# Two transformer blocks on one core: the even attention takes short and long token tiles in another order

## The reference

```python
def diff_attend(q, k, v, lam):
    s = jnp.einsum('bqhmd,bkhmd->bhmqk', q, k) * (A_QK ** -0.5)
    p = jax.nn.softmax(s, axis=-1)
    a = p[:, :, 0] - lam * p[:, :, 1]
    return jnp.einsum('bhqk,bkhd->bqhd', a, v)
```

## Time and profile before

| | |
|---|---|
| median of 3 runs | 2235.92 us (2234.37 to 2238.08) |
| profiled execution, its span | 2237.9 us |
| mean granted clock of TensorE | 0.982 |
| busy in the span: TensorE | 2167.8 us (97%) |
| busy in the span: VectorE | 1361.6 us (61%) |
| busy in the span: ScalarE | 559.2 us (25%) |

### The profile page before, as it was taken

One profiled execution on the slowest core, in us unless ns is written; L12 is line 12 of the kernel. 1 busy time (PEld: TensorE's weight loads), 2 busy tenths in 40 slices (PEclk: granted clock), 3 DMA queues, 4 the chain that ended last, 5 costly groups with the idle time before them and its releaser, 6 DMA issues.

```text
span 2237.9 us, 28630 instructions
## 1 busy us (share of the span) xinstructions
PE 2167.8 (97%) x12022; PEld 1779.8 (80%) x12022; DVE 1361.6 (61%) x1795; ACT 559.2 (25%) x1105; POOL 48.7 (2%) x31
## 2 busy tenths in 40 slices
PE   8999998899999999999999999999999999999998
PEld 5788885568788668887888888888888888888887
DVE  5124547985571474885787754554888437977633
ACT  4110006861221462374311110221100003111101
POOL 0000000000010020300000000000000000000000
PEclk9899997999799999999999999999999999999999
DMA  7233322312131012202222222222222232222322
GB/s 308 98 127 119 126 65 59 82 61 95 36 126 63 33 57 75 77 18 95 76 94 98 105 82 91 97 95 103 84 83 74 99 101 87 100 88 99 110 94 76
DMA packets 34241, 204.54 MB, mean 91 GB/s; under 512 B 4801, under 2 KB 5057, under 8 KB 14657
## 3 DMA queue, kind: packets, MB, share of 16 engines
q1 hardware_dynamic: 32736, 197.99, 25.4%
q10 hardware_dynamic: 1376, 4.72, 0.6%
HBM read 191.16 MB, written 2.10 MB: 86 GB/s over the span
## 4 chain that ended last, share of the span: by engine, by line
PE 86%; DVE 8%; ACT 3%; issue 2%; DMA 1%; DVEq 0%; SPq 0%; ACTq 0%
PE ps L437 23%; PE ps L438 22%; PE ps L439 22%; PE ps L536 3%; PE ps L538 3%; PE ps L537 3%; PE ps L691 2%; DVE stat L2236 2%; PE ps L585 1%; PE ps L1332 1%; PE ps L568 1%; PE ps L791 1%; PE ps L1024 1%; DVE h2lo L2062 1%; ACT prob L1568 1%
## 5 line engine op out<-in xcount | busy, mean ns | idle before, releaser
L1940 DVE CAST whi<-raw 128x2048 fp32r<-128x2048 f32 (+2 forms) x148 | 172.2, 1164 | 440.2 <-DMA raw<-in_ffn_out 107.7
L437 PE MATMUL ps<-h2hi,whi 128*128 128x512 f32 (+1 forms) x1084 | 416.9, 385 | 3.4 <-DVE h2lo L2062 3.0
L439 PE MATMUL ps<-h2hi,wlo 128*128 128x512 f32 (+1 forms) x1084 | 412.6, 381 | 0.0
L438 PE MATMUL ps<-h2lo,whi 128*128 128x512 f32 (+1 forms) x1084 | 412.5, 381 | 0.0
L1943 DVE TENSOR_TENSOR wlo<-raw,whi 128x2048 fp32r<-128x2048 f32 (+2 forms) x148 | 320.2, 2164 | 5.1
L437 PE MATMUL ps<-h1hi,whi 128*128 128x512 f32 (+1 forms) x768 | 271.7, 354 | 3.4 <-DVE h1lo L2144 1.4
L438 PE MATMUL ps<-h1lo,whi 128*128 128x512 f32 (+1 forms) x768 | 269.5, 351 | 0.0
L439 PE MATMUL ps<-h1hi,wlo 128*128 128x512 f32 (+1 forms) x768 | 267.5, 348 | 0.0
L437 PEld LDWEIGHTS ps<-h2hi,whi 128*128 128x128 f32 x1084 | 203.7, 188 | 44.6 <-DVE h2lo L2062 3.0
L439 PEld LDWEIGHTS ps<-h2hi,wlo 128*128 128x128 f32 x1084 | 203.7, 188 | 39.3
L438 PEld LDWEIGHTS ps<-h2lo,whi 128*128 128x128 f32 x1084 | 203.8, 188 | 37.7
(11 more groups left out here) (330 smaller groups left out, 3333.3 us busy)
## 6 DMA issues: line engine op xcount, KB each, us to landing
raw<-in_ffn_in SPq DMA_DIRECT2D x44, 1024.0 KB, 4.9
raw<-in_even SPq DMA_DIRECT2D x16, 1024.0 KB, 7.8
mod_w<-in_mod SPq DMA_DIRECT2D x6, 2048.0 KB, 19.1
raw<-in_odd SPq DMA_DIRECT2D x12, 1024.0 KB, 4.9
raw<-in_sgu_v SPq DMA_DIRECT2D x12, 1024.0 KB, 4.8
raw<-in_sgu_u SPq DMA_DIRECT2D x12, 1024.0 KB, 4.9
raw<-in_sgu_out SPq DMA_DIRECT2D x16, 768.0 KB, 4.2
raw<-in_ffn_out SPq DMA_DIRECT2D x16, 704.0 KB, 4.0
```

The lines of the kernel that those rows point to most:

```text
L437: pe.matmul(o, r(lhi), r(rhi), start=first, stop=False, **kw)
L438: pe.matmul(o, r(lhi), r(rlo), start=False, stop=False, **kw)
L439: return pe.matmul(o, r(llo), r(rhi), start=False, stop=last, **kw)
L1940: step(dve.tensor_copy(whi[:, slot, 0:width].bitcast(F32R), raw[:, slot, 0:width]))
```

## The change

`EVEN_T` sets the order of tiles in a pair to 4, 0, 5, 1, 2, 3: two short units, two long ones, two short ones, six long ones. What was tied to a tile number is tied to the place in the pair (u % 12). `EVEN_SLOT` gives the place of a tile's result in bank 7, so that part 0 of the output copy (four tiles, now 4, 0, 5, 1) is one instruction that reads the places in another order, and part 1 takes tiles 2 and 3. `SUM_AT` keeps each unit's sum in its old column. The head sums go to bank 5, and are made with unit 4 of a pair; the first scores that use this bank again wait for the variance. The convolved parts go from the pair's unit 9 (the second head of tile 4, now gone from there) to unit 9 of the new order, and the variance to unit 4. The first scores wait for `zed`, the second for `sg_in`, the third for `b_read`, which was the wait of the first. As the last unit is long now, its early blocks are copied behind the loop.

```diff
@@ -310,7 +310,10 @@
         sg = {k: sem(f"sgu_{k}") for k in ("v", "moments", "root", "normed", "gelu", "gated",
                                            "rowsum", "ws", "rows_copied", "uhalf")}
 
-        EVEN_UNITS = [(hp, t, a) for hp in range(4) for t in range(6) for a in range(2)]
+        EVEN_T, EVEN_SLOT = (4, 0, 5, 1, 2, 3), (1, 0, 3, 2, 0, 1)
+        EVEN_UNITS = [(hp, t, a) for hp in range(4) for t in EVEN_T for a in range(2)]
+        long_units = [sum(t < 4 for _, t, _ in EVEN_UNITS[:u + 1]) for u in range(len(EVEN_UNITS))]
+        SUM_AT = [32 + 12 * hp + 2 * t + a for hp, t, a in EVEN_UNITS]
         EVEN_MOVES = [2 if t < 4 else 1 for _, t, _ in EVEN_UNITS]
         moved = [sum(EVEN_MOVES[:u]) for u in range(len(EVEN_UNITS) + 1)]
         ROPE = [(side, j) for j in range(4) for side in range(2)]
@@ -321,7 +324,7 @@
 
         def head_sums_at(t):
 
-            return ps[:, 2, 256:268] if t < 3 else ps[:, 6, 0:12]
+            return ps[:, 5, 256:268] if t < 3 else ps[:, 6, 0:12]
 
         WITH_PREV = [sum(1 for v in range(u) if v % 4) for u in range(17)]
         SWA_TILES = [u + WITH_PREV[u] for u in range(17)]
@@ -778,12 +781,14 @@
 
                 hp, t, a = EVEN_UNITS[u]
                 b = 3 * (u % 2)
-                if t == 0 and a == 0:
+                if u % 12 == 0:
                     pe.wait_ge(ea["stack"], 384 * (hp + 1))
                 if u >= 2:
                     pe.wait_ge(ea["exp"], 2 * (u - 1))
-                if t == 0 and a == 0 and hp >= 2:
-                    pe.wait_ge(ea["var"], hp - 1)
+                if u == 2:
+                    pe.wait_ge(b_read, 4)
+                if u % 12 == 7 and hp:
+                    pe.wait_ge(ea["var"], hp)
 
                 def term(o, m, i, k0, n):
                     rows = slice(64 * m, 64 * m + 64)
@@ -797,7 +802,7 @@
                             first.then_inc(ea["bank_shared"], 1)
                         term(ps[:, b + 2, :], 1, i, 256, 512)
                     term(ps[:, b, :], 0, 0, 0, 512)
-                    pe.wait_ge(ea["bank_shared"], 8 * hp + 2 * t + a + 1)
+                    pe.wait_ge(ea["bank_shared"], long_units[u])
                     for i in range(2):
                         term(ps[:, b + 1, 256:512], 1, i, 0, 256)
                     last = term(ps[:, b, :], 0, 1, 0, 512)
@@ -811,16 +816,17 @@
 
                 hp, t, _ = EVEN_UNITS[2 * p]
                 kts = (range(3 * half, 3 * half + 3), range(4 + half, 5 + half))[t >= 4]
+                slot = EVEN_SLOT[p % 6]
                 if half == 0:
                     pe.wait_ge(ea["copied"], moved[2 * p + 2])
-                    if t == 4:
+                    if p % 6 == 4:
                         pe.wait_ge(ea["out"], 2 * hp + 1)
-                    elif t == 0 and hp:
+                    elif p % 6 == 0 and hp:
                         pe.wait_ge(ea["out"], 2 * hp)
                 for kt in kts:
                     for a in range(2):
                         h = 2 * hp + a
-                        last = pe.matmul(ps[64 * a:64 * a + 64, 7, t % 4 * P:t % 4 * P + P], ev[:, kt, h * 64:h * 64 + 64],
+                        last = pe.matmul(ps[64 * a:64 * a + 64, 7, slot * P:slot * P + P], ev[:, kt, h * 64:h * 64 + 64],
                                          ept[(2 * p + a) % 4][:, kt, :], start=kt == (0 if t < 4 else 4), stop=kt == 5)
                 if half:
                     last.then_inc(ea["pv"], 1)
@@ -842,15 +848,16 @@
                                      blk[:, 0:P:64], start=True, stop=True)
                 last.then_inc(ea["sums"], 1)
 
-            pe.wait_ge(b_read, 4)
+            pe.wait_ge(zed, 4)
             even_scores(0)
+            pe.wait_ge(sg_in, 4)
             even_scores(1)
             pe.wait_ge(mod_ready, 8)
             last_unit = len(EVEN_UNITS) - 1
             for u, (hp, t, a) in enumerate(EVEN_UNITS):
                 if u < last_unit - 1:
                     even_scores(u + 2)
-                if (t, a) == (4, 0) and hp:
+                if u % 12 == 4 and hp:
                     head_sums(hp - 1, head_sums_at(hp - 1))
                 if u:
                     even_transposes(u - 1, range(4, 6), moved[u] - 1)
@@ -1567,7 +1574,7 @@
                 at = m * (TA if t < 4 else 512)
                 act.activation(prob[u % 3][:, m, 0:n], flat[:, at:at + n], ACT.Exp,
                                bias=stat[:, 2 * (u % 4) + m:2 * (u % 4) + m + 1],
-                               accum_out=stat[:, 8 + u % 4:9 + u % 4] if m else stat[:, 32 + u:33 + u])\
+                               accum_out=stat[:, 8 + u % 4:9 + u % 4] if m else stat[:, SUM_AT[u]:SUM_AT[u] + 1])\
                     .then_inc(ea["exp"], 1)
 
             def even_copy(u, late):
@@ -1583,8 +1590,12 @@
 
             def even_out(hp, part):
                 act.wait_ge(ea["pv"], 6 * hp + (4, 6)[part])
-                cols = (slice(0, TX), slice(TX, TA))[part]
-                tell(copy(eot[:, hp, cols], ps[:, 7, 0:(TX, TC)[part]]), ea["out"], 2 * hp + part + 1)
+                if part == 0:
+                    to = eot[:, hp, :].rearrange("p (j i n) -> p j i n", i=2, n=P)[:, 0:3:2, :, :]
+                    last = copy(to, ps[:, 7, :].rearrange("p (i j n) -> p j i n", i=2, n=P))
+                else:
+                    last = copy(eot[:, hp, 256:512], ps[:, 7, 0:256])
+                tell(last, ea["out"], 2 * hp + part + 1)
 
             even_exp(0, 0)
             even_exp(0, 1)
@@ -1598,13 +1609,14 @@
                     even_copy(u - 1, 1)
                 if u < last_unit:
                     even_exp(u + 1, 1)
-                if (t, a) == (0, 0) and hp < 3:
+                if u % 12 == 0 and hp < 3:
                     even_hi(hp + 1)
-                if (t, a) == (1, 0) and hp:
+                if u % 12 == 2 and hp:
                     even_out(hp - 1, 1)
                     even_square(hp - 1)
-                elif (t, a) == (5, 0):
+                elif u % 12 == 10:
                     even_out(hp, 0)
+            even_copy(last_unit, 0)
             even_copy(last_unit, 1)
             act.preload_act_table(ACT.Sqrt)
             even_out(3, 1)
@@ -2257,20 +2269,19 @@
                 i = u % 4
                 dve.wait_ge(ea["exp"], 2 * u + 2)
                 step(dve.reciprocal(stat[:, 12 + i:13 + i], stat[:, 8 + i:9 + i]))
-                step(dve.scalar_tensor_tensor(out=stat[:, 16 + i:17 + i], in0=stat[:, 32 + u:33 + u], scalar=lam4[:, 3:4],
+                step(dve.scalar_tensor_tensor(out=stat[:, 16 + i:17 + i], in0=stat[:, SUM_AT[u]:SUM_AT[u] + 1], scalar=lam4[:, 3:4],
                                               in1=stat[:, 12 + i:13 + i], op0=ALU.mult, op1=ALU.mult))
                 p = prob[u % 3]
                 dve.scalar_tensor_tensor(out=p[:, 0, 0:n], in0=p[:, 1, 0:n], scalar=stat[:, 16 + i:17 + i],
                                          in1=p[:, 0, 0:n], op0=ALU.mult, op1=ALU.add).then_inc(ea["probs"], 1)
                 if u + 2 < len(EVEN_UNITS):
                     even_max(u + 2)
-                if (t, a) == (0, 1) and hp < 3:
+                if u % 12 == 1 and hp < 3:
                     even_lo(hp + 1)
-                if (t, a) == (4, 1):
-                    if hp:
-                        head_variance(hp - 1)
-                    if hp < 2:
-                        convolved_parts(hp)
+                if u % 12 == 4 and hp:
+                    head_variance(hp - 1)
+                if u % 12 == 9 and hp < 2:
+                    convolved_parts(hp)
 
             convolved_parts(2)
             convolved_parts(3)
```

## The result

The changed kernel takes 2254.98 us (median of 6 runs; five lie between 2247.88 and 2258.48, the sixth took 4665.37 and is left out of the ratio) beside 2238.0 us for the kernel before on the same chip. The ratio is 1.0065 with a 95% interval of 1.0049 to 1.0081: slower by some 11 to 18 us. The forecast was 2240.6 us (2233 to 2246.5), so the direction was the expected one and the size was not. The profiled execution spans 2256.7 us with a mean granted clock of 0.977.

A forecast was written before the change was run, and what follows sets the result against it. VectorE was taken to set the pace of the even attention, with 11.1 us of waits to save at most. Waits -0.2, tail +3.1 and clock +1.8 gave +4.7 us on 2235.92: 2240.6 us, range 2233 to 2246.5.

The forecast's parts named there:

- clock, behind pair 0: Stage behind pair 0: one fall of TensorE's clock taken, +1.8 us, bounds 0 (none) and +8 (four).
- waits: VectorE's waits over the stage: 10.7 us after the change against 10.9 before, a gain of 0.2 us.
- tail, net of work done earlier: Stage end, now long units: 10.35 us to the first output product against 5.08, less 2.13: +3.1 us.
- the one at 385: In the kernel before: TensorE's 1.75 us wait next to the convolved parts, after which the clock fell.
- rival B: TensorE's work in thinner pieces, clock falls once a pair, four falls at about 2 us: 2247 us; chance 0.2.
- price for a fall: Ahead of the pair boundary 1.8 us against 0.83 before; after the first short couple, at the head sums, 2 to 2.3.
- the walk: Engine-by-engine timelines of the stage: 3.8 us of waits for start and pair 0, 2.05 each in pairs 1 to 3.
- First scores and moved work: Stage start: earlier scores win 0.26 us; convolved parts, variance, DMAs, weight loads and strided copy taken at no cost.
- the signs that were named: VectorE's wait for TensorE 2.6 to 6 or 7 us, for ScalarE 8.3 to 3 to 5; tail about 10 us.
- Rival A: Short couples find TensorE free, waits 4.2 in place of 10.9: 2232.3 us, 2229 if the end is overlapped; chance 0.22.

The follow-up runs named there:

- more fillers: Changed kernel plus repeated value products and scores and small filler products where TensorE waits, in pairs 0 to 2: 2247.18 us, ratio 1.0029.
- all remedies: Changed kernel with last pair in old order, convolved parts at the next pair's unit 4, fillers in pairs 0 to 2 except at unit 10: 2236.0 us.
- head sums behind: Changed kernel with the head sums issued behind the transposes and value product of their turn instead of ahead: 2250.95 us, ratio 1.0066.
- parts at unit 4: Changed kernel with the convolved parts of pairs 0 and 1 moved from unit 9 to unit 4 of the next pair: 2246.68 us, ratio 1.0039.
- the moved line in the old order: Kernel before with the convolved parts of pairs 0 and 1 at unit 8 instead of 9: 2234.55 us, ratio 0.9975; again 2236.65 us, 0.9994.

## Why the prediction was wrong

The 16.1 us that the stage grew by, set against the terms of the forecast's sum. As measure of the full clock I take the run with more fillers for pairs 0 to 2 (its extra products make the clock's share here a lower bound, and the waits' an upper one) and the first profile of the changed kernel for pair 3.

| term | forecast | shown |
|---|---|---|
| clock, behind pair 0 | +1.8 (0 to +8) | +9.2: pair 1 3.7, pair 2 3.8, tail 1.6 |
| waits | -0.2 | +3.7: pair 0 +2.3, pairs 1 and 2 -0.4, pair 3 +1.8 |
| tail, net of work done earlier | +3.1 | +3.2 |

**The clock: the step that failed.** 41.1 and 39.7 us against 37.4 and 35.8 with fillers, and 11.6 against 10.0 in the tail. In the second profile of the changed kernel it is 3.8 and 2.0 in pairs 1 and 2 and 3.1 in pair 3, 8.9 in all. Both are above my upper bound. I had the places: some 1.6 us of waiting behind the convolved parts, 1.3 and 0.95 around the low parts (2.00, 1.26 and 0.92 came). But I took them as one fall for the whole stage, "as the two waits lie shorter or further apart than the one at 385", and there were two in each of pairs 1 and 2. A fifth came in the tail (in the second profile, in pair 3). That is rival B's mechanism, which had 0.2 and 2247 us, and still more falls than it had. Its price for a fall was about right where a fall comes early in the pair (2.03 - 0.65 = 1.4 at unit 14) and too low at the head sums: 1.31 + 0.88 + 1.23 + 0.76 is 4.2 us where the walk had 0.37 + 0.42 + 0.37, so 3.0 in place of 2 to 2.3.

**How long a wait has to be.** By the Trainium skill (TensorE: Matmul & The Clock Gate, HAM oscillation) TensorE should have no idle stretch of several microseconds. The forecast took this as the only case in which the clock falls and set it aside for the 1.75 us wait of before (the slow level begins at 384.85, some 1.3 us into that wait). The runs side with the row: in the version with all remedies no wait of more than 0.65 us stands in the 35 us ahead of the slow stretch at 390.3. They don't give a length that decides it either. In the five profiles with both places of waiting untouched (the changed kernel twice, first scores as before, last pair in the old order, head sums behind), a slow stretch begins during the boundary wait of 1.88 to 2.05 us or within 2.1 us of its end ten times out of ten, and another begins within 5.5 us of the waits around the low parts each time. With shorter waits it comes in one pair and not in the next.

**Waits at full clock: a second error, of 4 us.** In the first profile about 1 us of it is in pair 0, where the walk had 3.8 us of waits at the slow clock; in the second profile pair 0 is 0.8 us shorter and this part is gone. Another 1.2 us is in pairs 1 and 2, where the measure is the upper bound named above. The largest part, 1.9 us, is in pair 3. Its maxima of the third and seventh unit wait 0.58 and 0.38 us as the walk had it (0.65 and 0.37). The first of them:

```profile
471.03 1.76 DVE L2248 TENSOR_REDUCE stat<-ps 128x2 f32<-128x1536 f32 x1 [0.58 <-PE ps L796]
```

The place missed is on ScalarE:

```profile
477.37 0.39 ACT L1380 ACTIVATE eot<-ps 128x256 f32<-128x256 f32 x1
477.79 0.84 ACT L1380 ACTIVATE esq<-eot 128x768 f32<-128x768 f32 x1
478.54 0.58 ACT L1380 ACTIVATE ept<-ps 128x512 f32<-128x512 f32 x1
```

```profile
480.52 0.17 DVE L2271 RECIPROCAL stat<-stat 128x1 f32<-128x1 f32 x1 [0.93 <-ACT prob L1575]
```

The output copy and the squares of the pair before, 1.2 us at the pair's unit 2, used to have long units on both sides. Now the second short couple comes right behind them, and the small steps of its first unit, which I had at 0.24, wait 0.93. In pairs 1 and 2 the low parts on VectorE cover that. I had taken these two as unmoved work and not walked past them. Another wait was missing, 0.41 at the pair's first unit, and that behind the head sums is 0.60 in place of 0.42 (the walk's own terms give 0.37). In all, waits of 0.15 us or more in pair 3 are 3.5 us where they were 2.1. The rest, some 0.4 us, isn't in smaller gaps, which sum to 0.8 us both times; where a wait comes behind an instruction the overlap with the next one is lost (a short combination takes 0.46 us to its successor, the wait aside, and took 0.41).

**The tail: right, with a small slip.** The sum took 2.13 us off for work not yet done and left out that the variance, 0.40 us, is done earlier now; the tail itself came 0.3 us shorter than walked, and the two cancel. 10.35 us forecast, 10.04 measured at full clock, 11.60 in the profile in which a slow stretch began at 503.5. The last maximum and the first output product there:

```profile
497.78 1.75 DVE L2248 TENSOR_REDUCE stat<-ps 128x2 f32<-128x1536 f32 x1
```

```profile
509.38 0.50 PE L440 MATMUL ps<-h1hi,whi 128*128 128x512 f32 x1
```

**First scores and moved work: right.** 0.26 us at most was expected of the earlier scores; their run shows none: the first maximum starts 2.29 us behind the same product of VectorE with them and without. The strided output copy, the stacks' DMAs and the split panels show no wait of their own.

**Of the signs that were named**, the tail, the first maximum that doesn't follow the earlier scores, and the several waits of maxima on scores came. Those waits were 12.5 us instead of 6 to 7, which alone says that the clock term was off, and the waits for ScalarE stayed at 8.3 instead of 3 to 5. Rival A (the short couples find TensorE free) is excluded by the 0.58 at full clock ahead of a pair's third maximum.

**What stays open.** Why slow stretches sit in other places from one execution of a kernel to the next isn't shown, nor why the same waits bring one in one pair and not in the next. The stage's start goes with the time that TensorE had at the slow clock ahead of it: 4.0 us for a start at 338.4, 13.7 for 342.2, 34.1 for 350.8. Why that time differs isn't shown. A new order at full clock throughout was not reached: the best version had one slow stretch, and by the estimate above it would only draw level with the moved line in the old order.

## What to carry over

Before interleaving short and long units, list where the tensor engine will wait for another engine. Take every such place of about 2 us as a fall of the clock with a price in the slack-free stretch behind it, and don't average over them; one of about a microsecond can bring a fall too. What makes that wait (here 1.5 us of unrelated vector work) is better placed where the vector engine itself waits: such a move took 10 us off the stage in the one profile of it in the new order (the ratio of the whole kernel went from 1.0070 to 1.0039, some 7 us, with intervals that overlap), and 3 to 4 us in the old one. The last unit's length is a latency that nothing covers: end a pipeline on its short units.

## What the runs showed of the hardware

- The granted clock went down behind single waits of TensorE of 1.88 to 2.05 us, ten times out of ten. Behind waits of 1.26 and 0.92 us with 1.7 us of work between them it fell ten times out of ten where such a long wait stood a few us ahead, and in the one profile without it (parts at unit 4) it fell once, 6.5 us later, and once not at all. Behind 0.60, 0.44 and 0.65 us it fell in pair 1 and stayed in pair 2 (all remedies). Behind 0.47 and 0.61 us (parts at unit 4) it stayed.
- Adding matrix products shortened the kernel's stage: 252 instead of 184 recorded products in pair 0 and 2.6 us less.
- The price of a slow stretch depends on the schedule: 0.9 us for twelve slow microseconds in the old order, 2.3 to 3.1 us for ten in the new.
- The head sums, recorded as twelve products of two columns each, take 1.50 us at the full clock and 2.72 at the slow one.
